# First unit of a fused conv decoder step: tokens in four chunks, each with both column blocks and the whole contraction

## The reference, cut to what matters

```python
z = rmsnorm(h, norm_g)
proj = jnp.einsum('btd,de->bte', z, w_in)
a_val, a_glu, a_gate, b_h, b_c, b_b, b_gate, m_a, m_b = jnp.split(proj, SPLIT_IDX, axis=-1)
...
y_a = jax.nn.silu(c_a) * jax.nn.silu(a_gate)
```

## Time and profile before

| | |
|---|---|
| runs | 1175.93, 1176.33, 1176.99 us (median 1176.33) |
| the profiled execution | 1175.6 us, span in the trace 1173.8 us |
| PE busy | 1055.5 us, 90% of the span |
| DVE, ACT, POOL busy | 762.7, 460.1, 601.6 us |
| moved by DMA | 212 MB, 181 GB/s on the mean |

### The profile page before, as it was taken

The page is one execution under the profiler, slowest core; times in us unless marked ns, Lnnn a source line. Parts: engine busy times, 40 slices in busy tenths (PEclk is TensorE's granted clock), DMA queues, the critical chain, the costliest instruction groups (busy, mean ns, idle before and its releaser), DMA issues.

```text
span 1173.8 us, 19871 instructions
## 1 busy us (share of the span) xinstructions
PE 1055.5 (90%) x7948; PEld 1024.7 (87%) x7948; DVE 762.7 (65%) x816; ACT 460.1 (39%) x694; POOL 601.6 (51%) x451
## 2 busy tenths in 40 slices
PE   4868999999999999999998888895966986997997
PEld 4868999999999999999998888895966976996885
DVE  5635979899999999898845436330661384646333
ACT  7334343433434444344344444461541252222221
POOL 2155666565656565665745555543754564545000
PEclk8888999999999999999999999888988988998999
DMA  7446575666656667565688879988669877764220
GB/s 258 107 118 139 129 196 128 181 153 164 164 146 171 157 162 173 143 174 144 160 245 223 236 207 271 282 238 285 168 190 282 226 187 213 198 235 163 91 90 37
DMA packets 217583, 212.24 MB, mean 181 GB/s; under 512 B 10799, under 2 KB 171055, under 8 KB 216452
## 3 DMA queue, kind: packets, MB, share of 16 engines
q1 hardware_dynamic: 192724, 165.88, 44.5%
q0 software_dynamic: 24768, 45.10, 21.4%
HBM read 131.83 MB, written 35.00 MB: 142 GB/s over the span
## 4 chain that ended last, share of the span: by engine, by line
PE 64%; DMA 12%; issue 5%; DVE 4%; POOL 4%; ACT 3%; SPq 2%; ACTq 0%; DVEq 0%; POOLq 0%
PE pp L1816 55%; PE pp L1968 8%; POOL wop L837 4%; DMA m_spill<-big 3%; DMA ring<-in_w_in_dram 2%; DMA ring<-ring 2%; DMA big<-mb_spill 2%; DVE big L1529 2%; DMA ga_spill<-big 1%; DVE big L1531 1%; SPq L433 1%; ACT xop L932 1%; ACT wop L906 1%; DMA mb_spill<-big 1%; DMA big<-yb_spill 1%
## 5 line engine op out<-in xcount | busy, mean ns | idle before, releaser
L1816 PE MATMUL pp<-xop,wop 128*128 128x262 f32 (+1 forms) x7224 | 913.6, 289 | 82.9 <-ACT big L1060 61.2
L1816 PEld LDWEIGHTS pp<-xop,wop 128*128 128x128 f32 x7224 | 906.4, 194 | 88.0 <-issue 82.9
L837 POOL TENSOR_TENSOR wop<-ring,wop 128x512 fp32r<-128x512 f32 (+1 forms) x262 | 455.2, 1745 | 367.5 <-ACT wop L906 367.1
L906 ACT ACTIVATE wop<-ring 128x512 fp32r<-128x512 f32 (+1 forms) x262 | 182.0, 698 | 271.5 <-PE pp L1816 258.1
L1512 DVE TENSOR_TENSOR big<-big,pp 128x524 f32<-128x524 f32 (+1 forms) x43 | 29.9, 694 | 121.6 <-PE pp L1816 120.8
L1432 DVE SCALAR_TENSOR_TENSOR big<-big,cst 128x513 f32<-128x513 f32 x112 | 104.7, 935 | 0.6
L1968 PE MATMUL pp<-xop,wop 128*128 128x512 f32 x384 | 91.3, 400 | 6.7 <-DVE wop L1766 6.7
L1968 PEld LDWEIGHTS pp<-xop,wop 128*128 128x128 f32 x384 | 73.4, 192 | 24.3 <-issue 6.9
L1443 DVE SCALAR_TENSOR_TENSOR spare<-big,tap_sum,spare 128x512 f32<-128x512 f32 x112 | 83.7, 748 | 0.3
L1432 DVE SCALAR_TENSOR_TENSOR spare<-big,cst,spare 128x512 f32<-128x512 f32 x112 | 83.6, 746 | 0.0
L1347 DVE TENSOR_TENSOR xop<-big,xop 128x2064 fp32r<-128x2064 f32 (+1 forms) x21 | 54.0, 2592 | 41.6 <-ACT xop L932 41.5
(11 more groups left out here) (119 smaller groups left out, 674.4 us busy)
## 6 DMA issues: line engine op xcount, KB each, us to landing
ring<-in_w_in_dram SPq DMA_DIRECT2D x249, 256.0 KB, 3.5
ring<-ring POOLq DMA_DIRECT2D x172, 256.0 KB, 4.5
big<-c_spill SPq DMA_DIRECT2D x16, 516.0 KB, 6.7
ring<-in_w_pb_dram SPq DMA_DIRECT2D x28, 256.0 KB, 4.2
ring<-in_w_pa_dram SPq DMA_DIRECT2D x28, 256.0 KB, 3.6
big<-yb_spill SPq DMA_DIRECT2D x5, 1032.0 KB, 11.3
big<-ya_spill SPq DMA_DIRECT2D x5, 1032.0 KB, 11.8
yb_spill<-big SPq DMA_DIRECT2D x8, 516.0 KB, 5.4
```

Source lines behind the costliest of these rows:

```text
L837: G.tensor_tensor(wop[:, s0:s1, 1, :], raw, f(wop[:, s0:s1, 0, :]), ALU.subtract).then_inc(wlo, 1)
L906: A.activation(wop[:, s0:s1, 0, :], raw, ACT.Copy).then_inc(whi, 1)
L1816: last = T.matmul(out, wop[:, s, wp, P * k:P * (k + 1)], xop[s][:, xp, k, n * ch:n * (ch + 1)], start=(s in FRESH and k == 0 and m == 0), ...
```

## The change

Unit 0 is cut by tokens instead of by contraction halves. There are four chunks (`CHUNKS0`): tokens 16 to 270, 270 to 524, 524 to 786, 786 to 1048. Each takes both blocks and the whole contraction: four products of 12 matmuls, of 254 columns in the first two chunks and 262 in the others. The 16 meta tokens are left out of the gate, which does not need them.

Each operand quarter is split in two pieces (`first_high`, `first_low`), each as soon as the tiles of its chunk are there: three tiles for the first chunk, then five, seven and nine. Tiles 0 to 3 are transposed ahead of the products, tiles 4 to 8 and the constants between them. Both PSUM banks of a chunk are read by one swish; its buffer now lies over weight slots 2, 4 and 6, which unit 0 does not use, so that unit 1's weights for these slots wait for the store. Tiles 2, 3, 7 and 8 move forward in SP's list of loads, the constants and three weights move back.

The quarters' sums go in another order (operands 2 to 5 are named by other quarters), and the high parts for operands 2 to 5 are made in the order 3, 2, 4, 5: those of 3 and 2 on ACT before unit 1's copies, between unit 1's first three weights; the last sum `x_sum(0, 3)` moves from unit 1 to DVE's list before it.

```diff
-    X0 = {0: 1, 1: 2, 6: 3, "21": 4, 4: 5, 2: 6, 3: 7, 5: 8}
+    X0 = {0: 3, 1: 4, "21": 7, 6: 8, 3: 9, 2: 10, 4: 11, 5: 12}
...
+    CHUNKS0 = ((0, META, MID), (0, MID, HZ), (1, 0, CZ), (1, CZ, HZ))
...
-        first = [x_stage[:, 4 + r, 0:HZ] for r in range(4)]
+        first = []
+        for c, (_, a, b) in enumerate(CHUNKS0):
+            at = (2 * 2 * W, 2 * 2 * W + 2 * (MID - META), 4 * 2 * W, 6 * 2 * W)[c]
+            first.append(w_stage[:, at:at + 2 * (b - a)].rearrange("p (r n) -> p r n", r=2))
...
-        X_SRC = ((0, 1, 0, 2, 4, 1, 3), (0, 1, 0, 3, 2, 1, 0))
+        X_SRC = ((0, 1, 3, 4, 0, 1, 3), (0, 1, 0, 3, 2, 1, 0))
...
-        USED0 = {0: 6, 1: 4, 3: 7, 5: 5}
+        PLAIN = (0, 1, 3, 5)
+        USED0 = {0: 12, 1: 13, 3: 14, 5: 15}
...
+                    for c in {2: (0, 1), 3: (2,), 6: (3,)}.get(s0, ()):
+                        act.wait_ge(out0[c], 16)
...
+            def first_high(c, kh):
+
+                act.wait_ge(zf_dve if kh else zf_act, tiles_of(c))
+                A.activation(plain_x(c, kh)[:, 0, :, piece(c)], quad(0, 2 * CHUNKS0[c][0] + kh)[:, :, piece(c)], ACT.Copy)\
+                    .then_inc(xhi, 1)
```

In unit 1, ACT then copies the first product, takes `x_high(0, 4)`, `w_hi(1, 5)`, the next unit's first two weights and `x_high(0, 5)`. DVE's list ends before unit 1 with `x_sum(0, 0)`, `x_sum(0, 1)`, `x_low(0, 3)`, `x_low(0, 2)`, `x_sum(0, 2)`, `x_sum(0, 3)`. PE's list is:

```diff
-            for i in range(7):
+            for i in range(4):
                 transpose_x(i)
...
+            for c in range(4):
+                plain_product(c, 0)
+                plain_product(c, 1)
+                if c < 3:
+                    transpose_x(4 + 2 * c)
+                else:
+                    transpose_consts()
+                plain_product(c, 2)
+                plain_product(c, 3)
+                if c < 2:
+                    transpose_x(5 + 2 * c)
```

More of the change, by code:

```diff
@@ L173, in decoder_step @@
             xop[s] = sb(f"xop{s}", [P, 2, KH, HZ], F32R)
+        with nc.sbuf_tensor("w_stage", [P, SLOTS * 2 * KH * P], F32) as w_stage:
+            pass
         wop = sb("wop", [P, SLOTS, 2, KH * P], F32R)
@@ L507, in load_ga @@
                     sp.wait_ge(sqacc, K)
-                    sp.wait_ge(out0[j], 16)
-                    sp.wait_ge(out0[2 + j], 16)
+                    for r in range(4):
+                        sp.wait_ge(out0[r], 16)
                 else:
@@ L901, in w_hi @@
                 raw, s0, s1 = w_step(v, n)
-                if v == 1 and s0 in USED0:
-                    act.wait_ge(prod, prod_at(0, USED0[s0]))
+                if v == 1:
+                    if s0 in USED0:
+                        act.wait_ge(prod, prod_at(0, USED0[s0]))
+                    for c in {2: (0, 1), 3: (2,), 6: (3,)}.get(s0, ()):
+                        act.wait_ge(out0[c], 16)
                 elif v > 1:
@@ L952, in z_evacuate, with first_swish @@
                 A.activation(zf[:, 0:KH, P * i:P * i + n], src, ACT.Copy).then_inc(zf_act, 1)
[L954 to L963, removed]
+            def first_swish(c):
+                act.wait_ge(prod, prod_at(0, 4 * c + 3))
+                n = CHUNKS0[c][2] - CHUNKS0[c][1]
+                A.activation(first[c], first_bank(c)[:, :, 0:n], ACT.Silu).then_inc(swish0, 1)
+            root_mean_square(0)
+            root_mean_square(1)
+            root_mean_square(2)
             z_evacuate(0)
@@ L968, in _ @@
             w_hi(0, 1)
+            z_evacuate(2)
+            first_high(0, 0)
+            first_high(0, 1)
+            w_hi(0, 2)
             root_mean_square(4)
-            z_evacuate(2)
+            w_hi(0, 3)
+            z_evacuate(3)
             root_mean_square(5)
-            z_evacuate(3)
+            z_evacuate(4)
+            first_high(1, 0)
+            first_high(1, 1)
             root_mean_square(6)
[L974 to L977, removed]
+            z_evacuate(5)
             root_mean_square(7)
             root_mean_square(8)
-            w_hi(0, 3)
-            for i in range(5, XT):
-                z_evacuate(i)
+            z_evacuate(6)
+            first_high(2, 0)
+            first_high(2, 1)
+            act.wait_ge(sq_done, XT)
             first_swish(0)
+            z_evacuate(7)
+            first_swish(1)
+            z_evacuate(8)
+            first_high(3, 0)
+            first_high(3, 1)
+            first_swish(2)
             act.wait_ge(cst_t, 1)
@@ L1358, in x_sum @@
                     if n == 1:
[L1359 to L1365, removed]
+                        dve.wait_ge(xlo, 8)
+                    out, x, y, op = ((q[4], q[2], q[3], ALU.subtract), (q[3], q[4], q[0], ALU.subtract),
+                                     (q[0], q[0], q[2], ALU.subtract), (q[1], q[3], q[1], ALU.add))[n]
                 else:
```

162 lines of the change are left out of this document (78 added, 84 removed).

## The result

The changed kernel took **1165.53 us** on the median of four runs (1163.49 to 1166.54), the kernel before 1176.13 over four: ratio 0.9913, 95% interval 0.9886 to 0.994. A second series (under e7) gives 0.9888 [0.9859, 0.9916].

The account below looks back on a forecast made before the run. PE, busy 1055.5 of 1173.8 us, was taken as the bound, with gains only up to slot 5. That slot comes 9.1 us earlier, 8.9 from the first unit: 1175.6 less 9.1, plus 0.7, gives 1167.2 us; range 1162 to 1172.5.

Parts of the forecast that it names:

- Rival 4: Later units or front loads: something absorbs the gain or a load order costs it, leaving 1176 us; chance 0.06.
- rival 3: First unit: all 192 products run at the low clock, 247 ns each, ending 14.8 us later, 1191 us; chance 0.05.
- Start: First unit's front: with three tiles and half a quarter needed, the first product starts at 18.3 us instead of 25.43.
- Loads "at nothing": SP's load list at the start: moving tiles, weights and constants was priced at no cost or gain.
- Length of the first unit: PE's list from first product to the unit's end: products 5.9 and 20.7, transposes 5.0, bundles 1.4, sum 33.0 us.
- none at the lower level, 3.0 less: First unit's length, bound: if no products run at the lower clock instead of the first 24, 3.0 us less.
- What feeds it: ACT's work in the first unit: 19.7 us, done by 37.6, some 6 us in hand; first swish has the same slack.
- The second unit, from E: Waits counted from the first unit's end (E): slot 2 at E+15.9, slot 5 (the sixth) at E+33.4 instead of E+33.6.
- The price of 3.1 us for the covered splits: Second unit: POOL's splits of weights 1 and 2 under three DVE operations end at E+9.5 instead of E+6.4.
- Rival 1: Second unit: POOL's splits get through between DVE's operations, giving 3.7 us more, 1163.5 us; chance 0.14.
- Rival 2: Second unit: POOL kept out (+2.8), spill late (+1.6), add slow (+1.9); gain falls to 2.8 us, 1173.5; chance 0.11.
- A microsecond won at that slot should arrive at the end: Second unit's sixth slot (slot 5) to the end: time won there carries through, as later transfers are released by results.

Follow-up runs that it names:

- e7: The changed kernel timed and profiled anew with no edit, beside the kernel before: median 1161.94 us over six runs, ratio 0.9888.
- e1: The changed kernel with SP's loads (tiles 2, 3, 7, 8, constants, weights) back in the old order: 1166.47 us in one run.
- e4: The changed kernel with PE waiting for all four of the first unit's weights before its first product, instead of one: 1172.04 us in one run.
- e6: e2 plus, on ACT, the second unit's fourth-product copy before the next unit's third weight and first swish before sixth half piece; DVE's tap sum later: 1154.98 us.
- e2: The changed kernel with DVE's long operations held back until POOL has split the second unit's first three weights: median 1157.42 us, ratio 0.9867.
- e3: The changed kernel with ACT's fourth swish and the second unit's first-product copy ahead of the fourth weight: median 1165.93 us, ratio 0.9937.

## Why the prediction was right, and where it was not

**The time and the mechanism.** Predicted 1167.2, measured 1165.53 and 1161.94. The gain comes from the start, reaches PE's full stretch at slot 5, and stays at 12.6 us up to the marker; the two ratios, 0.9913 and 0.9888, make it 10 to 13 us at the end. Rival 4 (the time does not arrive) and rival 3 (clock stays low, slower) did not happen. But the sum was short by 3.4 us at slot 5 (9.1 against 12.50), and in the pair first seen nearly the same amount, 3.3, was lost later. The close hit owes something to that luck.

Three of the prediction's own signs came out otherwise: a gap of 1.61 us where none over 1 us was to be; a gain that is not one constant (12.50, 12.63, 9.2); and a clock below 1.00 beyond 30 us, 0.75 between 50 and 55 in the second unit, though before it was 0.74 there too, between 60 and 65.

**Start.** 18.3 predicted, 17.66 measured. Loads "at nothing" was off by 1.1 us in the change's favour; in the old order the first product comes at 18.80 (e1), 0.5 later than the sum. (The terms of the sum, 15.37 + 0.58 + 0.98 + 1.3, make 18.2.)

**Length of the first unit.** 33.0 predicted, 30.71 measured (48.37 - 17.66). The step that failed is "I take the first 24 products at the lower level, 5.9": they took 3.08, then 4.59 in e7. Of the eight profiles with the new front six have 3.08 or 3.09, behind a gap of 0.55 to 1.27 us, and e4 alone comes near the 5.9 of the sum, with 5.49, where PE had stood idle for 5.73 us. The bound named in the prediction, "none at the lower level, 3.0 less", is what the first profile shows. The transposes were mis-sized too: 1.04 to 1.09 instead of 1.26, 0.8 for four. Against these stand two waits of 1.88 in all that the sum had at nothing.

**What feeds it.** "The first swish ... has the same slack" was wrong. It stood behind a half piece that waited 0.70 us for DVE, and its table (1.28) then lay on PE's path: 1.61. I had added ACT's work as a sum, done early enough by the end, and had not followed the one instruction that PE waited for. e6 takes the cause away, and E comes 1.15 earlier.

**The second unit, from E.** Here each step is borne out within 0.6 us:

| step | predicted | measured |
|---|---|---|
| slot 0 | E+3.0 | E+2.76 |
| three splits done on POOL | E+9.5 | E+9.39 |
| slot 2 | E+15.9 | E+15.35 |
| first add of the next unit | E+21.1 | E+20.67 |
| second add | E+27.1 | E+26.57 |
| next unit's weight on ACT | E+30.3 | E+29.76 |
| slot 5 | E+33.4 | E+32.98 |

The price of 3.1 us for the covered splits, taken from a row late in the trace, was right, and e2 shows the cause. Rival 1 (POOL gets through between DVE's operations) fell: the three splits under DVE's list took 2.90, 3.37 and 3.39 us, none 1.3. Rival 2 needed the store and the add to be slow: the store was issued at 62.59 and did not hold the sixth weight at 65.31; the second add went out 5.90 after the first (69.04 to 74.94), where the sum had 6.0 (5.5 and 0.5).

**What arrives.** "A microsecond won at that slot should arrive at the end" holds to the marker in every version that still has a stop at slot 5 (from there to the marker 509.5 to 510.8 us). Behind it both PE's waits and its busy time for the same 3406 matmuls (481.7 us in e2, 488.5 in e3) change from one execution to the next: 567.4 to 573.1 us over ten profiles. "0.2%, what a measurement can tell from no change" was too small for single runs of this kernel, which spread over 11 us.

**What stays open.** Of the eight profiles with the new front, six have 571.9 to 573.1 behind the marker and two 567.4 and 569.6; the two of before have 568.3 and 569.4. Whether the new front makes the long case more frequent, at some 3 us, is not settled by ten profiles. It does not grow with the gain: e4, 6.3 us ahead of before at the marker, has 572.1, e6, 23.2 ahead, has 573.1. No edit to the late units was tried. Why the first 24 products ran at two levels in the same kernel is open as well.

## What to carry to other kernels

Follow each instruction that PE waits for through its own engine's list, one by one; a sum of an engine's work says only that it could be in time. Where DVE and POOL work on SBUF at the same time, price each at what a row shows them to take together, and let DVE wait if POOL's result is the one on the path. When an early gain has been worked out, look for it at a marker in mid-span before judging it by the end, where the time scatters by more than the gain of a single edit.

## What the hardware showed that was not expected

- A POOL split of 128x512 took 1.26 us with DVE waiting and 3.2 us beside DVE's operations with two inputs, and DVE's own took 2.80 instead of 2.30 (4.59 for two).
- The same 24 products at the same place took 3.08 us in one execution and 4.59 in another of the same kernel, both after a gap of 1.26 us behind the transposes; the granted clock between 15 and 20 us was 1.00 and 0.79. After a gap of 5.73 us it was 0.50 and they took 5.49.
- An add by DMA was usable 3.3 us after its issue (57.71 to 61.01; in e2 52.06 to 55.36), and 4.6 us after it (57.64 to 62.20 in e3) where a load was issued 0.08 us behind it.
- The same 3406 matmuls behind the marker kept PE busy for 485.87 us in one execution and 487.65 in another of the same kernel.
